# Sample attention of a hybrid decoder step: two sequences' scores and two heads' values side by side in the array

## The reference

```python
def attn_sample(q1, q2, k, v, lam, k_pages, v_pages, page_table):
    n, t = q1.shape[:2]                              # 8 sequences, 8 new tokens
    past = page_table.shape[1] * PAGE_SIZE           # 2 pages of 128
    k_past = k_pages[page_table].reshape(n, past, N_HEADS, 2 * HEAD_DIM)
    v_past = v_pages[page_table].reshape(n, past, N_HEADS, V_DIM)
    ...
    return diff_attend(q1, q2, k_all[..., :HEAD_DIM], k_all[..., HEAD_DIM:], v_all, q_pos, k_pos, lam)

def diff_attend(q1, q2, k1, k2, v, q_pos, k_pos, lam):
    ...
    s1 = einsum('nqhd,nkhd->nhqk', q1, k1) * scale + bias
    s2 = einsum('nqhd,nkhd->nhqk', q2, k2) * scale + bias
    w = softmax(s1, axis=-1) - lam * softmax(s2, axis=-1)
    return einsum('nhqk,nkhv->nqhv', w, v)
```

## Time and profile before

| what | value |
|---|---|
| median of 3 executions | 1138.55 us |
| lowest and highest of them | 1136.86 and 1142.63 us |
| span of the profiled execution | 1136.5 us |
| PE busy | 1025.5 us, 90% of the span |
| DVE, ACT, POOL busy | 687.1, 527.1, 229.8 us |
| sample stage, from its first matmul to the next stage's first | 388.57 to 431.32 us |

### The profile page before, as it was taken

The page is one execution under the profiler, slowest core; times in us unless marked ns, Lnnn a source line. Parts: engine busy times, 40 slices in busy tenths (PEclk is TensorE's granted clock), DMA queues, the critical chain, the costliest instruction groups (busy, mean ns, idle before and its releaser), DMA issues. The chain is left out here.

```text
span 1136.5 us, 17850 instructions
## 1 busy us (share of the span) xinstructions
PE 1025.5 (90%) x5490; PEld 844.9 (74%) x5491; DVE 687.1 (60%) x1361; ACT 527.1 (46%) x902; POOL 229.8 (20%) x552
## 2 busy tenths in 40 slices
PE   7999999998999998999981799999999999999920
PEld 5877889888677786688861588888888888888710
DVE  4547558241789526476548656544666798686438
ACT  4233333423688726322212245543555778576334
POOL 0623556800200000000000012121231213213110
PEclk9999999999899999999985799999999999999965
DMA  7230241213740243733320876667969799997355
GB/s 241 61 102 28 81 127 35 69 38 105 260 162 1 72 140 130 285 112 128 128 69 18 315 259 232 190 209 258 293 222 332 262 339 377 359 327 256 111 151 200
DMA packets 52289, 201.34 MB, mean 177 GB/s; under 512 B 10146, under 2 KB 16162, under 8 KB 46082
## 3 DMA queue, kind: packets, MB, share of 16 engines
q1 hardware_dynamic: 41714, 138.43, 34.3%
q0 software_dynamic: 7488, 27.27, 10.1%
q10 hardware_dynamic: 3024, 34.87, 7.9%
HBM read 163.80 MB, written 36.73 MB: 176 GB/s over the span
## 5 line engine op out<-in xcount | busy, mean ns | idle before, releaser
L2154 DVE TENSOR_TENSOR wlo<-raw,whi 128x1024 fp32r<-128x1024 f32 x192 | 221.6, 1218 | 35.9 <-ACT whi L2051 35.1
L2051 ACT ACTIVATE whi<-raw 128x1024 fp32r<-128x1024 f32 x184 | 179.3, 1049 | 31.3 <-PE psG L1996 19.5
L1994 PE MATMUL psG<-whi,exs 128*128 128x512 f32 x200 | 81.9, 410 | 7.0 <-DVE wlo L2154 5.3
L1994 PE MATMUL psY<-whi,ehs 128*128 128x512 f32 x200 | 81.0, 405 | 4.3 <-DVE wlo L2154 4.3
L1959 POOL DMA_INDIRECT acc<-eyb,idxs x25 | 40.6, 1622 | 195.8 <-ACT eyb L2069 195.8
L1996 PE MATMUL psG<-whi,exs 128*128 128x512 f32 x200 | 79.3, 396 | 0.0
L1995 PE MATMUL psG<-wlo,exs 128*128 128x512 f32 x200 | 79.0, 395 | 0.0
L1996 PE MATMUL psY<-whi,ehs 128*128 128x512 f32 x200 | 78.7, 393 | 0.0
L1995 PE MATMUL psY<-wlo,ehs 128*128 128x512 f32 x200 | 78.7, 393 | 0.0
L1996 PE MATMUL psU<-whi,exs 128*128 128x512 f32 x200 | 78.1, 390 | 0.0
L1994 PE MATMUL psU<-whi,exs 128*128 128x512 f32 x200 | 77.8, 389 | 0.0
(11 more groups left out here) (406 smaller groups left out, 2319.9 us busy)
## 6 DMA issues: line engine op xcount, KB each, us to landing
raw<-in_moe_w_gate SPq DMA_DIRECT2D x16, 2048.0 KB, 9.3
raw<-in_moe_w_up SPq DMA_DIRECT2D x16, 2048.0 KB, 10.1
raw<-in_moe_w_down ACTq DMA_DIRECT2D x16, 2048.0 KB
early<-in_w_in SPq DMA_DIRECT2D x27, 256.0 KB, 3.7
stg<-in_x_prompt SPq DMA_DIRECT2D x8, 512.0 KB, 4.2
kc<-in_cache_k SPq DMA_DIRECT2D x16, 256.0 KB, 3.0
vc<-in_cache_v SPq DMA_DIRECT2D x16, 256.0 KB, 3.2
mr<-in_w_out SPq DMA_DIRECT2D x8, 512.0 KB, 3.3
```

The costliest lines, as they stand in the source:

```text
L1994: pe.matmul(out, hi, w_hi, start=(k == 0), stop=False)
L2051: nc.scalar.activation(whi[:, at], s.raw[:, at], ACT.Copy).then_inc(hi_made[i], 1)
L2154: nc.vector.tensor_tensor(wlo[:, at], s.raw[:, at], whi[:, at].bitcast(F32), ALU.subtract) \
```

## The change

The scores of the eight sequences are no longer accumulated into all 128 rows with zeros for the others. Rows are ordered anew: rows 0 to 63 belong to the even sequences, 64 to 127 to the odd ones, each with 16 rows of its own (8 of the first kind, 8 of the second). `qm` has 64 columns per sequence, and a score matmul writes 64 rows: even sequences the lower half of the bank's partitions, odd ones the upper half. The constants for bias, `two` and `sel` follow the new order, and so does `qf`; POOL writes both with other strides, in more and smaller copies.

`values` takes two heads at once, head h in partitions 0 to 63 of its bank and head h+1 in 64 to 127 of its own, with their matmuls in turn. Pairs of head 2 stand ahead of the values of heads 0 and 1, those of head 3 between the two calls. There are four `own` and four `new`, two of the `own` in the space of the queries of heads 2 and 3 (`s.qT[2]`, `s.qT[3]`), so that `keep_pairs` does not wait for sums. The diff, with the renaming of views left out:

```diff
@@ attend, POOL @@
-                nc.gpsimd.memset(s.qm[:, :, :, :], 0.0).then_inc(zeroed, 1)
+                nc.gpsimd.memset(s.qm, 0.0).then_inc(zeroed, 1)
...
-                        nc.gpsimd.tensor_copy(s.qf[r, h, NS * j:NS * j + NS], s.qT[h][r, SEQ:N])
-                        for bh in range(2):
-                            dst = own_columns(s.qm, r, h, 4 * bh, NS * j + T_DEC * 4 * bh)
-                            nc.gpsimd.tensor_copy(dst, s.qT[h][r, SEQ + 32 * bh:SEQ + 32 * bh + 32]
-                                                  .rearrange("p (b t) -> p b t", t=T_DEC))
+                        new = s.qT[h][r, SEQ:N].rearrange("p (c e t) -> p e c t", e=2, t=T_DEC)
+                        for e in range(2):
+                            every = s.qf[r, h, NS * e:NS * (e + 1)].rearrange("p (c x) -> p c x", x=2 * T_DEC)
+                            nc.gpsimd.tensor_copy(every[:, :, T_DEC * j:T_DEC * (j + 1)], new[:, e, :, :])
+                            nc.gpsimd.tensor_copy(own_columns(s.qm, r, h, e, j), new[:, e, :, :])
@@ sample @@
-        own = [sb(f"own{k}", [P, NB_DEC * STEP]) for k in range(2)]
+        own = [sb(f"own{k}", [P, NB_DEC * STEP]) for k in range(2)] + [s.qT[k] for k in (2, 3)]
...
-        new = [s.raw[:, V_AT + 2 * KC + NS * k:V_AT + 2 * KC + NS * (k + 1)] for k in range(2)]
+        new = [s.raw[:, V_AT + 2 * KC + NS * k:V_AT + 2 * KC + NS * (k + 1)] for k in range(H)]
...
-        psO = [psK[h][0:NS, 0:P] for h in range(H)]
+        psO = [psK[h][NS * (h % 2):NS * (h % 2) + NS, 0:P] for h in range(H)]
@@ POOL @@
-                for k in range(2):
+                for k in range(H):
                     nc.gpsimd.memset(own[k][:, :], 0.0).then_inc(m["zeroed"], 1)
@@ PE, scores @@
-                        pe.matmul(psS[h % 2][:, 0:PAST], qm[:, h, b, :], keys_of(h, b, 1),
-                                  start=(b == 0), stop=(b == NB_DEC - 1))
+                        pe.matmul(psS[h % 2][NS * (b % 2):NS * (b % 2) + NS, 0:PAST], qm[:, h, b, :],
+                                  keys_of(h, b, 1), start=(g == 0), stop=(g == 3))
@@ PE, values @@
-                def values(h):
-                    pe.wait_ge(m["pairs_kept"], h + 1)
-                    if h == 0:
+                def values(h0):
+                    both = (h0, h0 + 1)
+                    pe.wait_ge(m["pairs_kept"], h0 + 2)
+                    if h0 == 0:
                         pe.wait_ge(m["v_in"], 16 * NB_DEC * NPG)
-                    pe.matmul(psO[h], new[h % 2][0:NS, :], s.v[0:NS, QB, h * P:(h + 1) * P], start=True, stop=False)
+                    for h in both:
+                        pe.matmul(psO[h], new[h][0:NS, :], s.v[0:NS, QB, h * P:(h + 1) * P], start=True, stop=False)
                     for b in range(NB_DEC):
                         for j in range(NPG):
-                            last = pe.matmul(psO[h], own_page(h % 2, b, j), vc[:, NPG * b + j, h * P:(h + 1) * P],
-                                             start=False, stop=(b == NB_DEC - 1 and j == NPG - 1))
-                    last.then_inc(m["summed"], 1)
+                            done = b == NB_DEC - 1 and j == NPG - 1
+                            for h in both:
+                                last = pe.matmul(psO[h], own_page(h, b, j), vc[:, NPG * b + j, h * P:(h + 1) * P],
+                                                 start=False, stop=done)
+                                if done:
+                                    last.then_inc(m["summed"], 1)
@@ PE, order @@
-                    if h in (1, 2):
+                    if h >= 1:
                         pairs(h - 1)
                 values(0)
-                pairs(2)
-                values(1)
                 pairs(3)
                 values(2)
-                values(3)
@@ DVE @@
-                        dve.wait_ge(m["zeroed"], 2)
-                    if h >= 2:
-                        dve.wait_ge(m["summed"], h - 1)
+                        dve.wait_ge(m["zeroed"], H)
...
                 add_bias(3)
+                keep_pairs(2)
                 scale(3)
-                put_o(0)
-                keep_pairs(2)
-                put_o(1)
                 keep_pairs(3)
-                put_o(2)
-                put_o(3)
+                for h in range(H):
+                    put_o(h)
@@ own_columns @@
-def own_columns(qm, r, h, b0, at):
...
+def own_columns(qm, r, h, e, j):
+    at = (h * NB_DEC + e) * NS + j * T_DEC
+    step = 2 * (NS + T_DEC)
+    return qm[r, at:at + 4 * step].rearrange("p (c x) -> p c x", x=step)[:, :, 0:T_DEC]
@@ constants @@
-    seq, t = (r % NS) // T_DEC, r % T_DEC
+    first, t = r % (2 * T_DEC) < T_DEC, r % T_DEC
+    seq = 2 * (r % NS // (2 * T_DEC)) + r // NS
...
-    two = np.concatenate([np.eye(NS), np.eye(NS)], 0)
-    sel = np.stack([r < NS, r >= NS], 1).astype(np.float32)
+    two = (T_DEC * seq + t)[:, None] == np.arange(NS)[None, :]
+    sel = np.stack([first, ~first], 1)
@@ attention @@
-        s.qm = s.aT[:, :, :].rearrange("p h n -> p (h n)")[:, 0:H * NB_DEC * P] \
-            .rearrange("p (h b c) -> p h b c", h=H, b=NB_DEC)
+        s.qm = s.aT[:, :, :].rearrange("p h n -> p (h n)")[:, 0:H * NB_DEC * NS + 3 * NS]
```

More of the change, by code:

```diff
@@ L305, in sample @@
         sem = semaphores(nc, c)
-        kc, qm, qf = s.kc, s.qm, s.qf
+        kc, qf = s.kc, s.qf
+        qm = s.qm[:, 0:H * NB_DEC * NS].rearrange("p (h b c) -> p h b c", h=H, b=NB_DEC)
         vc = sb("vc", [P, NB_DEC * NPG, W])
@@ L431, in keep_pairs @@
                     if h == 0:
-                        dve.wait_ge(m["zeroed"], 2)
-                    if h >= 2:
-                        dve.wait_ge(m["summed"], h - 1)
-                    dst = own[h % 2][:, :].rearrange("p (b c) -> p b c", b=NB_DEC)[:, :, 0:NPG * NS] \
+                        dve.wait_ge(m["zeroed"], H)
+                    dst = own[h][:, :].rearrange("p (b c) -> p b c", b=NB_DEC)[:, :, 0:NPG * NS] \
                         .rearrange("p b (j c) -> p b j c", j=NPG)[:, :, :, 0:T_DEC]
@@ L439, in keep_pairs @@
                         nc.vector.tensor_copy(dst[:, :, j, :], src[:, :, j, :])
-                    nc.vector.tensor_copy(new[h % 2][0:NS, :], psP[h % 2][0:NS, 2 * NS:3 * NS]) \
+                    nc.vector.tensor_copy(new[h][0:NS, :], psP[h % 2][0:NS, 2 * NS:3 * NS]) \
                         .then_inc(m["pairs_kept"], 1)
```

## The result

The changed kernel took 1133.55 us (median of 6 runs, 1130.06 to 1136.74) beside 1138.89 for the one before in the same series: a ratio of 0.9950 with a 95% interval of 0.9932 to 0.9968, so 5.3 us less by the medians and 5.7 (3.6 to 7.7) by the ratio, where 8.6 less was forecast. Two more series of the unchanged pair gave 4.6 and 8.2 us less by the medians, with ratios of 0.9954 and 0.9937.

A forecast was written before the change was run, and what follows sets the result against it. TensorE's work was taken to bound the sample-token attention stage, then the cached values' DMA. The terms ended the stage at 421.99 instead of 430.57; 8.6 us off the 1138.55 median gave 1130.0 us, range 1127 to 1135.

The forecast's parts named there:

- Turns and shapes: Key transposes between scores: 1.21 us a turn instead of 1.30, shape changes included; with later scores, 3.1 us earlier.
- The bound moves to the DMA: Before the values: TensorE ready at 409.8, waits for cached values until 411.05; only 1.0 of 3.1 us gained.
- The packed rate: Values of two heads in two column groups: 0.055 us per instruction instead of 0.109, 64 instructions in 3.72 us.
- The new wait and the tail: TensorE waits about 0.6 us for DVE's copies of head 3's pairs; the tail takes 1.19 us instead of 0.73.
- What was costed at nothing: GpSimd memsets and small copies, reordered DVE copies, SP's gate-weight wait, next-stage loads and the clock: no added time.
- The clock: In the stage: no fall expected from idles of 1.2 and 0.6 us; a fall for all values would cost 7 us.
- Behind the stage: Later stages: they keep their lengths, and the next stage's first instruction comes 8.6 us earlier.
- two heads ending together: Stage's tail: the second square must follow the first, 0.41 us plus about 0.05 for its wait.
- Program order: Rival, 9 in 100: a second group can't pass earlier instructions, three slots a turn; gain 7.0, 1131.5 us.
- No overlap in accumulation: Rival, 7 in 100: column groups accumulating in PSUM don't overlap, values keep 0.109 us; 4.1 later, 1142.6 us.
- a drain at each change of group: Rival, 6 in 100: each of some 90 column-group changes in scores and values costs 0.14 us; 16.7 later, 1155 us.
- a worse packed rate: Values at the upper bound of 0.060 us per instruction; counted as 0.6 us in the range's upper end.

The follow-up runs named there:

- one_group: Changed kernel with all four heads' sums in partitions 0 to 63, so one column group; ratio 0.9981 to the kernel before.
- kept_busy: Changed kernel with 14 unread transposes of cached keys between the pairs of head 2 and the values; ratio 0.9901 to the kernel before.
- scores_only: Kernel before with only the scores in two column groups, values, their order and buffers as before; ratio 1.0010.
- split_mid: Changed kernel with value-page landings on two semaphores and head 3's pairs inside the first values block; ratios 0.9899 and 0.9927 to the kernel before.
- busy_end: `split_mid` with nine unread transposes of cached keys behind the last values; 1125.97 us, ratio 0.9871 to the kernel before.

## Why the prediction was right or wrong

**Turns and shapes.** Right in sign, low in size. Two slots per turn, not three: 1.17 us against a worked-out 1.21. From the stage's first transpose to the product with the new keys of head 3 it is 19.40 us (386.73 to 406.13) against 23.23 before, so 3.8 earlier where 3.1 was said; 12 turns at 0.13 instead of 0.09 make 0.5 of the 0.7.

**The bound moves to the DMA.** Right: PE idles on the values' load, 1.58 us where 1.2 was said, since PE comes sooner. The values start 22.12 us behind the first transpose (22.20 and 22.50 in the other two traces) where 411.05 - 388.57 = 22.48 was said.

**The packed rate.** Right: the second block of 64 is 3.71 long, a step of (3.71 - 0.27) / 63 = 0.0546 on average, with the first start's extra time in it, where 0.055 was said. The open point of the prediction, packing with accumulation, has its answer. The 1.6 that was estimated from the Trainium skill's three-group figure ("TensorE: Matmul & The Clock Gate", Part 3) does not hold for two groups here: without one instruction's own 0.27 it is 6.93 in `one_group` against 3.44, a factor of 2.0.

**The new wait and the tail.** Right: from the pairs of head 3 to the last new-token products 1.49 us (414.41 to 415.90), 1.48 said; from the first last sum to the last square's end 1.22 (420.01 to 421.23), 1.19 said. What was costed at nothing shows nothing: in the list of waits of the stage DVE waits for no memset, and nobody for the gate weights but SP.

**The clock: the step that failed.** The step cited an idle of 2.07 us (2.04 by the timeline) with a clock of 1.00 behind it and expected no fall from shorter ones. One row was taken for a rule. Against the forecast the stage ended 1.1 us late, and it adds up so: landing 0.36 early, new-token products 0.62 instead of 0.36, the first block with its change of shape 4.94 (409.47 to 414.41) instead of 3.72, the rest within 0.1. The lower clock thus cost 0.26 + 1.22 = 1.5. `kept_busy` shows that the idle brings it. The prediction did name the case, for all of the values and 7 us; its true size was 1.5.

**Behind the stage.** The prediction let the later stages keep their lengths. The next stage was longer where the clock fell at its start: 172.5 in the mean of the changed kernel's three traces against 171.2 in the two of before. With the stage's 35.4 (mean of three) this makes 42.75 - 35.4 - 1.3 = 6.1 us, between the timed 4.6 and 8.2 and close to their mean of 6.0. What the prediction costed at 0.46, two heads ending together, also lengthens PE's idle at the barrier from 1.52 to 1.99; that this idle brings the fall is likely, and not proved. The rest can't be told from spread: the parts outside the stage differ by up to 5 us between traces of one kernel, and the stage's first transpose alone comes anywhere from 386.73 to 391.17 in the three traces of the changed kernel.

**The rivals.** Program order: against it stands the turn of 1.17, and the row at 398.75, where a score instruction (of the upper half, since the pairs hold the lower one) begins ahead of the last pairs' instruction (398.85), which stands before it in the code. The Trainium skill's strict order of matmuls ("TensorE: Matmul & The Clock Gate", Part 3, "The mechanism") is thus not what the starts of two column groups show here. No overlap in accumulation, and a drain at each change of group: both are excluded by 64 instructions in 3.71 us.

**Time.** 1133.55 against 1130.0, within 1127 to 1135. That it lies inside is in part luck: the upper end was made of starts in program order, a worse packed rate and spread. The first two did not come; the fall of the clock in the stage (1.5) and the longer next stage (1.3), for which the sum had no term, took their room. The chance of 0.79 for more than half a per cent was too high: by the ratios the three series gave 0.50, 0.46 and 0.63%, so the gain lies about on that bound.

## What to carry to other kernels

Matmuls that fill only 64 of the output partitions can run two at a time if they write to the two halves of the partitions; count the overlap from a row of the same kernel, and the changes of shape into and out of it, which cost 1.17 - 2 x 0.217 - 4 x 0.11 = 0.30 us in each turn here. Before costing such a gain, look for the transfer that was just in time: a faster engine meets it as a wait, and a second semaphore, so that the first half of the transfer counts by itself, took most of that wait away here (1.58 to 0.48 us). An idle of TensorE costs more than its length where the clock falls behind it, so a gain that opens an idle like the 1.58 us here has to be costed with the work behind it at the lower rate too. Where such a wait has to stay, work that nobody reads can pay: in `kept_busy` it made the stage 1.4 us shorter.

## What the runs showed of the hardware that was not expected

The granted clock fell behind each of the four idles of 1.58 to 1.96 us inside the stage (three traces of the changed kernel, one of `one_group`), and behind none of 0.61 us or less. At the barriers the same lengths gave either: of 14 traces, 4 had the lower clock in the stage's first transposes, behind idles of 1.76 and 1.77 us, while the other ten, with 1.75 to 2.04, had the full one; and 7 had it at the start of the next stage, behind 1.99 to 2.07, where two others with 1.99 and 2.00 had not. What tells these apart stays open. One thing goes with the four falls at the stage's start (`scores_only` and all three traces of `split_mid` and `busy_end`): there the clock had come up late in the stage before, too, with a mean of 0.61 to 0.63 over the first 16 us of `attend`, where the other ten traces have 0.68 to 0.72. `attend` took 103.95 to 104.04 us in these four, and 102.83 to 103.71 in the ten. Why that should matter at the end of `attend`, some 100 us later, is not shown. A loss there is not always seen: in `scores_only` the wait for the DMA took it in.
